# Norms of the second block, chunk by chunk: squares as units end, the inverse made with tokens on partitions, first panels with chunks outermost

## What is computed

```python
def rms_norm(x, g):
    y = x * lax.rsqrt(jnp.mean(x * x, axis=-1, keepdims=True) + NORM_EPS)
    return y * g
def modulate(h, shift, scale):
    return h * (1 + scale) + shift
...
for i in range(2):                      # second block; sh, sc, g from c; csh, csc, cg from c_ctx
    h_lat = modulate(rms_norm(x, norm_mix[i]), sh1, sc1)
    h_ctx = modulate(rms_norm(ctx, norm_mix[i]), csh1, csc1)
    y_lat, y_ctx = mixer(h_lat, h_ctx)  # i == 0: even_mixer; i == 1: odd_mixer, no y_ctx
    x = x + g1 * y_lat
    x = x + g2 * squared_relu_mlp(modulate(rms_norm(x, norm_mlp[i]), sh2, sc2), w1[i], w2[i])
    if i == 0:
        ctx = ctx + cg1 * y_ctx
        ctx = ctx + cg2 * squared_relu_mlp(modulate(rms_norm(ctx, norm_mlp[i]), csh2, csc2), ...)
```

## Time and profile before

| | us |
|---|---|
| time of three runs: median (lowest to highest) | 2420.59 (2417.02 to 2424.26) |
| the profiled execution, its own time | 2415.48 |
| its span, first to last instruction | 2413.8 |
| PE busy | 2198.2 (91%) |
| DVE busy | 1464.5 (61%) |
| ACT busy | 808.0 (33%) |

### The profile page before, as it was taken

The page is one execution under the profiler, slowest core; times in us unless marked ns, Lnnn a source line. Parts: engine busy times, 40 slices in busy tenths (PEclk is TensorE's granted clock), DMA queues, the critical chain, the costliest instruction groups (busy, mean ns, idle before and its releaser), DMA issues.

```text
span 2413.8 us, 38835 instructions
## 1 busy us (share of the span) xinstructions
PE 2198.2 (91%) x14936; PEld 1869.6 (77%) x14936; DVE 1464.5 (61%) x2446; ACT 808.0 (33%) x1241; POOL 38.3 (2%) x60
## 2 busy tenths in 40 slices
PE   7999849999999999899949899789999959997998
PEld 7999826999999998899937576567887836456987
DVE  6666566766666667766573556665255364566854
ACT  4444323444444444344312344211121103232332
POOL 0000000000000000000010000000000000000000
PEclk9999966999999999899979999989999979898999
DMA  7666400666566553466622110122322212002544
GB/s 266 229 217 218 151 0 36 225 229 211 203 247 230 179 194 106 142 231 237 216 103 70 36 36 24 71 70 87 104 87 101 91 49 91 18 18 85 176 169 145
DMA packets 50217, 325.74 MB, mean 135 GB/s; under 512 B 5328, under 2 KB 8656, under 8 KB 16976
## 3 DMA queue, kind: packets, MB, share of 16 engines
q1 hardware_dynamic: 42480, 266.62, 31.9%
q0 software_dynamic: 7648, 57.91, 6.4%
HBM read 323.45 MB, written 1.05 MB: 134 GB/s over the span
## 4 chain that ended last, share of the span: by engine, by line
PE 82%; DVE 12%; ACT 3%; issue 2%; DMA 0%; DVEq 0%; ACTq 0%; SPq 0%; PEldq 0%
PE psum L1629 17%; PE psum L1631 16%; PE psum L1630 16%; PE psum L1716 3%; PE psum L1717 3%; PE psum L1718 3%; PE psum L2131 3%; PE psum L1733 2%; DVE w_lo L850 1%; PE psum L1754 1%; PE psum L1995 1%; PE psum L2132 1%; DVE h_lo L1038 1%; DVE scratch L1051 1%; ACT scratch L667 1%
## 5 line engine op out<-in xcount | busy, mean ns | idle before, releaser
L529 ACT ACTIVATE w_hi<-raw 128x1024 fp32r<-128x1024 f32 (+1 forms) x542 | 514.0, 991 | 699.0 <-PE psum L1631 451.2
L1629 PE MATMUL psum<-h_hi,w_hi 128*128 128x256 f32 (+1 forms) x2256 | 683.2, 303 | 70.7 <-DVE h_lo L1038 60.8
L850 DVE TENSOR_TENSOR w_lo<-raw,w_hi 128x1024 fp32r<-128x1024 f32 (+1 forms) x542 | 599.6, 1148 | 220.6 <-ACT w_hi L529 202.9
L1630 PE MATMUL psum<-h_lo,w_hi 128*128 128x256 f32 (+1 forms) x2256 | 672.1, 298 | 0.0
L1631 PE MATMUL psum<-h_hi,w_lo 128*128 128x256 f32 (+1 forms) x2256 | 671.8, 298 | 0.0
L1629 PEld LDWEIGHTS psum<-h_hi,w_hi 128*128 128x128 f32 x2256 | 435.6, 193 | 106.5 <-issue 62.7
L1630 PEld LDWEIGHTS psum<-h_lo,w_hi 128*128 128x128 f32 x2256 | 435.8, 193 | 10.9
L1631 PEld LDWEIGHTS psum<-h_hi,w_lo 128*128 128x128 f32 x2256 | 435.4, 193 | 11.2
L1716 PE MATMUL psum<-g_both,w_hi 128*128 128x256 f32 x704 | 202.5, 288 | 2.0 <-DVE w_lo L850 1.9
L1717 PE MATMUL psum<-g_both,w_hi 128*128 128x256 f32 x704 | 199.1, 283 | 0.0
L1718 PE MATMUL psum<-g_both,w_lo 128*128 128x256 f32 x704 | 199.0, 283 | 0.0
(11 more groups left out here) (314 smaller groups left out, 3121.1 us busy)
## 6 DMA issues: line engine op xcount, KB each, us to landing
raw<-in_weights SPq DMA_DIRECT2D x207, 1024.0 KB, 4.9
raw_ada<-in_ada POOLq DMA_DIRECT2D x48, 1024.0 KB, 6.3
raw<-in_weights SPq DMA_DIRECT2D x64, 704.0 KB, 4.1
arena<-in_rpb POOLq DMA_DIRECT2D x1, 2048.0 KB, 9.7
arena<-in_fox_c POOLq DMA_DIRECT2D x1, 1888.0 KB, 9.3
const_region<-in_latent_c POOLq DMA_DIRECT2D x1, 1394.0 KB, 6.6
const_region<-in_even_c POOLq DMA_DIRECT2D x1, 1360.0 KB, 7.9
x_res<-in_x_lat SPq DMA_DIRECT2D x4, 256.0 KB, 7.1
```

Of the source, the lines that this page charges most:

```text
L529: nc.scalar.activation(wh[s][:, a], raw[s][:, a], ACT.Copy).then_inc(hi_ready, 1)
L850: V.tensor_tensor(wl[s][:, a], raw[s][:, a], wh[s][:, a].bitcast(F32), ALU.subtract).then_inc(lo_ready, 1)
L1629: mm(out, sh, mh, start=n == 0, stop=False)
L1630: mm(out, sh, ml, start=False, stop=False)
```

## The change

Norms A to D become five jobs in a table, `NORMS`. Job 0 is A for the context, job 1 A for the latent tokens, jobs 2, 3 and 4 are B, C and D.

- **Squares** go to ACT (`b_square`), one chunk at a time, as soon as the unit before has been added into `x`; DVE adds up the first 7 (6 for D) of them (`b_add`). Job 0 runs wholly inside ffn 3's second half: squares at q = 0 and 1, root at q = 4, inverse at q = 5, scaling at q = 7 to 15. Job 1's squares go there too.
- **The inverse** is made with tokens on partitions: `b_sums` multiplies each 128-token tile of the squares (as stationary operand) by two columns, so that 2 or 4 columns of means come out; ACT takes the root of them, DVE the reciprocal (128x2 or 128x4), and spreads each over the diagonal of a 128x128 tile. `b_broadcast` multiplies these by the matrix of 1/1024, which puts the inverse on all partitions, in PSUM.
- **Scaling** (`b_apply`): DVE scales from PSUM into four `b_t` buffers (`b_scale`), ACT makes `hh` with the shift as bias (`b_hi`), DVE makes `hl` (`b_low`). Semaphores `hl_ready` and `hc_ready` count chunks.
- **First panels**: PE runs the chunks outermost and waits for each. Both units of the panel then end together. In `even` the first panel is "first" in the order: context half of unit 0, `b_sums(1)`, context half of unit 1, `b_broadcast(1)`, then the latent halves chunk by chunk.
- ffn 3's second half and the second MLP's second half are unrolled on PE (16 and 8 panels in straight code), and the table of roots is loaded on ACT in `even` and `latent` during the output units.

```diff
+        NORMS = [dict(layer=0, which=0, name="norm_mix", cols=slice(T, TJ), slot=0, adds=7, r_bank=6,
+                      items=[(c, 1) for c in range(DC)], ...),
...
+            def b_square(n, c):
+                job = NORMS[n]
+                if c > 1:
+                    act.wait_ge(b_acc_done, job["n_acc"] + c - 1)
+                nc.scalar.activation(job["sq"][c % 2], x[:, c, job["cols"]], ACT.Square).then_inc(b_sq_made, 1)
+            def b_hi(n, items):
...
+                    act.wait_ge(b_t_made, g + 1)
+                    nc.scalar.activation(hh[:, c, who_cols(w)], b_t[:, g % 4, :], ACT.Identity,
+                                         bias=mods[:, col, w:w + 1]).then_inc(b_hi_made, 1)
...
                     hi_next(q, 0, 1, pos.e + q, SLOT if q == 15 else FH * P, between)
+                    if f == 3 and q < 2:
...
+                        for c in range(4 * q, 4 * q + 4):
+                            b_square(0, c)
+                    if f == 3 and q == 4:
+                        b_root(0)
+                    if f == 3 and 7 <= q <= 14:
+                        b_hi(0, (q - 7,))
...
+            def b_scale(n, i):
...
+                V.scalar_tensor_tensor(b_t[:, g % 4, :], x[:, c, who_cols(w)], gmod[:, job["slot"] + w, c:c + 1],
+                                       psum[:, job["r_bank"], who_cols(w)], ALU.mult, ALU.mult).then_inc(b_t_made, 1)
+            def b_low(n, i):
...
+                V.scalar_tensor_tensor(hl[:, c, who_cols(w)], b_t[:, g % 4, :],
+                                       mod(job["layer"], 3 * job["which"], c, w), hh[:, c, who_cols(w)].bitcast(F32),
+                                       ALU.add, ALU.subtract).then_inc(hc_ready if w else hl_ready, 1)
...
+                    if f == 3 and q >= 7:
+                        if q < 15:
+                            b_scale(0, q - 7)
+                        if q > 7:
+                            b_low(0, q - 8)
...
-            mod_norm(0, 1, (0, 1))
-            mlp_joint()
-            mlp_joint()
-            mod_norm(1, 0, (0, 1))
+            b_inverse(2)
+            b_apply(2)
+            mlp_joint(False)
+            mlp_joint(True)
             latent()
-            mod_norm(1, 1, (0,))
+            b_inverse(4)
+            b_apply(4)
...
+                if isinstance(i, int) and i == 0 and j == 0:
...
+                    for k in range(DC):
+                        pe.wait_ge(hl_ready, DC + k + 1)
+                        pe.wait_ge(hc_ready, DC + k + 1)
+                        for m in range(2):
+                            ins = three(psum[:, (pos.u + m) % 2, :], s, k, m, slice(0, TJ))
```

More of the change, by code:

```diff
@@ L254, in loop @@
         def loop(eng, n, body, peel):
-            if peel:
-                body(0)
+            for i in range(int(peel)):
+                body(i)
             if n > peel:
@@ L331, in unit @@
                 yield "b", n
+            yield "first", 0
             for n in range(8):
-                yield from unit(n)
+                if n > 1:
+                    yield from unit(n)
                 if n in (1, 2, 3, 4, 5, 7):
@@ L569, in body @@
                         if leads:
-                            square_root()
+                            (then or square_root)()
                         if extra:
@@ L675, in even @@
                 for what, k in even_order():
-                    if what == "a":
+                    if what == "first":
+                        lat_square(7)
+                        hi_next(0, 0, 1, pos.e, SLOT, lambda: b_root(1))
+                        b_hi(1, range(DC))
+                        pos.p += 1
+                        unit_of[0], unit_of[1] = pos.u, pos.u + 1
+                        pos.u += 2
+                        pos.e += 2
+                    elif what == "a":
                         if k % 2 == 0:
@@ new lines, in b_add, with b_inverse @@
+            def b_add(n, c):
+                job = NORMS[n]
+                dve.wait_ge(b_sq_made, 8 * n + c + 1)
+                if c == 0:
+                    ins = V.tensor_copy(job["acc"], job["sq"][0])
+                else:
+                    ins = V.tensor_tensor(job["acc"], job["acc"], job["sq"][c % 2], ALU.add)
+                ins.then_inc(b_acc_done, 1)
+                dve.wait_ge(b_acc_done, job["n_acc"] + c + 1)
+            def b_inverse(n):
+                job = NORMS[n]
+                r = small[:, 16:16 + job["tiles"]]
+                dve.wait_ge(b_rooted, n + 1)
+                step(V.reciprocal(r, r))
+                for t in range(job["tiles"]):
+                    V.tensor_scalar(b_diag[:, t, :], ident, r[:, t:t + 1], float(D), ALU.mult,
+                                    ALU.mult).then_inc(b_diag_made, 1)
@@ L1434, in place @@
                                       psum[:, s, :].rearrange("p (a b) -> p a b", a=2))
+                b_inverse(1)
+                b_apply(1)
                 for what, k in even_order():
-                    if what == "a":
+                    if what == "first":
+                        lo_next(0, 0, 1)
+                        pos.p += 1
+                        for n in range(2):
+                            evac_copies([place(n)(pos.u % 2)], pos.e + 1)
+                        b_gains(2)
+                    elif what == "a":
                         if k % 2 == 0:
```

268 lines of the change are left out of this document (221 added, 47 removed).

## The result

The changed kernel takes 2356.59 us (median of four runs, 2354.2 to 2357.3) against 2420.85 before (2417.02 to 2424.26). The ratio is 0.9733, with an interval from 0.9716 to 0.975: 64 us faster, where 75 had been forecast (2345, range 2329 to 2364). A second set of four runs gave 2355.61 (2347.9 to 2362.28).

What follows compares the result with a forecast made beforehand. PE, busy 91%, was taken to bound the kernel, with holes at four norms where DVE is the chain. Gains 25.5 + 22.6 + 13.6 + 22.5 = 84.2, less 9.0, gave 75.2 us: 2345 median, range 2329 to 2364.

Steps and rivals of the forecast that it cites:

- ffn 3's second half: Stage before norm A: added cost 9.0 us, from waits behind high parts (5.2), the inverse (0.7) and SP's queue (1.7).
- the untouched stages: Stages whose code the change leaves alone: the sum had no term for them, 0 us.
- The profiled execution would become 2340.3: Whole kernel: the profiled 2415.5 us less 75.2; runs' median 5.1 above it, so 2345.
- Norms B and C: Second block: B from 47.1 to 21.6 us, gain 25.5; C from 44.7 to 22.1, gain 22.6.
- PE follows DVE and even a slow first 4 us is made good: Norm B's first panel: a chunk takes PE 1.4 us, DVE 1.6, so PE's slow start costs nothing.
- Norm D: Half the tokens: from 27.7 to 14.1 us, gain 13.6; PE starts at 6.6, low part there at 13.4.
- Norm A: From 52.4 to 29.9 us, gain 22.5; 19.9 without the hold by POOL.
- The hold by POOL: Norm A: POOL's two additions hold DVE's first `b_low` until 19.9 us, costing 10 us.
- Rival (a): Norm A: POOL does not hold DVE, gain 10 us more, 2335; chance 0.18.
- Rival (c): ffn 3's second half costs more, ACT's queue behind for q = 7 to 15, clock partly low: 2362; chance 0.13.
- Rival (b): First panels: clock stays at the lower level; B +7.7, A +2.8, D +2.8, C nothing; 2358; chance 0.16.
- Rival (d): Unrolled PE stages: straight code not fetched fast enough, slower, 2425 at a pitch of 1.55; chance 0.01.

Runs made afterwards that it cites:

- POOL's additions moved: Changed kernel, POOL's two arena additions waiting behind norm A's last low part of h, or the second panel's weight low part: 2340.14 and 2338.9 us.
- units outermost: Changed kernel with the first panels' loops as before, unit 0 over all chunks, then unit 1, at A to D: 2352.93 us.
- the inverse of the whole tile: Changed kernel with squares summed into one whole tile, then root and reciprocal of it, as before, at B, C and D: 2351.66 us.
- the kernel with filling: Changed kernel with POOL's additions later, context high parts later, weight low parts earlier, and 128-column filler matmuls on PE at B and D: 2341.53 us.

## Why the prediction was right, and where it was off

The measured medians lie 11.6 and 10.6 us above the 2345 and inside the range, and the mechanism of the gain is the one forecast. That the sum came so near is in part luck: the four norms together gave 6.5 us less than forecast, ffn 3's second half cost 2.9 us less, and the two errors have nothing to do with each other.

**The largest term that failed is one that I did not write: the untouched stages, 0 against -9.6 us.** "The profiled execution would become 2340.3" takes it that these stages keep their times. They don't: the same instructions of "C to D" took 211.5 and 211.6 before, 216.1 and 216.2 in the changed kernel, 210.7 and 210.8 with POOL's additions moved, 219.4 with units outermost. 1.9 us of the 4.6 are the slow start of C's second panel, which my measure of a norm leaves out, as it ends at the second panel. 2.7 are lost 75 us later, where the clock falls in both kernels, but earlier and for longer in the changed one. Why it does is open: no experiment here moved one stage against time alone. The 3.2 us at the start are chance, as two traces of one kernel show; of the 3.2 in "A to B" 3.3 lie between two traces of the changed kernel, so their part is not settled.

**Norms B and C, 24.0 for 25.5 and 21.4 for 22.6.** DVE's 32 operations took 12.7 us, as forecast (12.8), but began late, and the last low part came at 19.5 instead of 18.4. 0.9 of that is the spreading, priced at 0.65 behind the last diagonal and 1.54 at the lower clock, and 0.2 the diagonals. (The upper price of 0.6 for a spreading call has no row; a call measured 0.26 at full clock and 0.52 at the lower.) At C that is the whole miss: the chain of gains, low part and reading came out as forecast, behind DVE. At B a second step failed, "PE follows DVE and even a slow first 4 us is made good". It was not made good: PE works without a wait to 22.8, DVE's own path would have ended near 22.6 (an estimate: its low part at 21.7, the reading 0.7, the handover 0.15), and taking the low part out of it left B at 23.0. The runs price the parts of the change: squares as units end 6.5 (at C), high parts on ACT 3.7 (at B), first product at the first chunk 3.8 (at D), units' order 2.9 (at B), the inverse by columns 0.2 to 1.2.

**Norm D, 11.1 for 13.6.** The sums ended at 4.0 instead of 3.3 and the spreading at 6.4 instead of 4.6, so PE began at 8.6 instead of 6.6. The panel then took 8.0 where the sum had 7.5, with 22 matmuls slow and the rest at full speed. It is PE that ends this norm, as forecast.

**Norm A, 21.1 for 22.5.** The hold by POOL was found; it was taken at 10 and costs about 8.5. Two other things were not foreseen. The sum has the context half at full clock (2.0 to 4.9), and it ran at the lower one, to 6.7. And POOL's load landed later, so that the additions began at 12.5, not at 10.7. The two delays are of nearly the same size, which is chance, and only so did both additions fall on low parts in full (with POOL's load 1.1 us sooner A was 28.7): POOL's addition started 0.01 us ahead of DVE's first low part in one trace and 0.07 us in the other. Rival (a), no hold, was wrong, and its price too: with units outermost the first low part did get ahead of POOL, the second one was held, and the last low part came 0.8 us sooner, not 10; with the inverse of the whole tile two got ahead, as the context half ran at full clock, and A was 1.9 shorter. One reading of the earlier trace rows was wrong: the single records show that the first of the two scalings ran its 0.48 us and the second was held, for 4.72; it began 0.3 us after POOL's second addition.

**ffn 3's second half, 6.1 for 9.0.** Four holes of 4.15 instead of 5.2; moving the high parts took away 4.3. The waits taken for the inverse at q = 5 (0.7) and SP's queue (1.7) show no hole of PE in the trace. Rival (c) was wrong.

**Rival (b), the clock in the first panels,** was half right. The panels start at the lower clock (22 matmuls at D), but are back within them. It costs 1.0 at B and 2.0 at D by the kernel with filling; the rival had 7.7 and 2.8 on top of a forecast that held 4 slow us. The Trainium skill (TensorE: Matmul & The Clock Gate, section HAM oscillation) warns of bursts that start slow again each time; at B, C and D no trace shows it. At A, where the hold splits the latent half, both bursts run at the lower clock, behind 6.43 and 3.00 idle us (a matmul of 256 columns every 0.21 us in both). Units outermost, which thins the bursts further, cost B 2.9 us, where its work alone was put at 2.7. Rival (d): the unrolled panels ran at 0.12 a matmul of 256 columns and 0.23 of 512, without a hole but for the four.

## What to carry to other kernels

Price a moved wait up to the point where the clock is back, not to the next panel: at norm C 1.9 us of slow start lie behind the point where my sum ended. And give the stages that a change leaves alone a range of their own: here they moved by 9.6 us in all. Before giving DVE a chain of instructions with two SBUF inputs, look for what POOL does with SBUF in that stretch (here 8.5 us), and put POOL's long instructions where DVE has only work that nobody waits for. And look twice at a step that replaces one long instruction by many short ones on PE: a spreading call costs 0.26 us, or 0.52 at the lower clock.

## What the runs showed of the hardware

- A matmul of 512 columns on f32 operands took 0.89 us at full clock, 3.9 times the 0.23 in fp32r.
- Two DVE instructions on 128x8, which read two operands in SBUF, took 6.95 us beside POOL's additions and 0.37 without them.
- A scaling with one operand in SBUF and one in PSUM was not held: with units outermost two took their usual 0.86 us inside POOL's second addition.
- A POOL instruction that waited for DVE was passed by DVE's next one with two inputs in SBUF: held over two halves of a low part, POOL's pair took 11.09 for 9.14.
- After the same wait of 1.78 us at full clock, PE's next 24 matmuls at norm A stayed at full clock in some programs (3.1 us) and fell to the lower one in others (4.6 us).
- Runs of one kernel fell on two levels 14 us apart, 2328 to 2329 and 2341 to 2344, with the mean clock at 0.96 and 0.953, and the runs show no cause.
